# Adaptive layer norm of the head in six shares of channels in place of four

## The reference

```python
mod = jax.nn.silu(c) @ ada_w[i] + ada_b[i]            # ada_w is 2048 x 12288
sh1, sc1, g1, sh2, sc2, g2 = jnp.split(mod[:, None, :], 6, axis=-1)
mod_c = jax.nn.silu(c_ctx) @ ada_w[i] + ada_b[i]
...
h = modulate(rms_norm(x, norm1_g[i]), sh1, sc1)       # h * (1 + scale) + shift
hc = modulate(rms_norm(ctx, norm1_g[i]), csh1, csc1)
proj = h @ w_in[i]
```

## Time and profile before

| | |
|---|---|
| time, median of 3 runs (lowest to highest) | 1738.75 us (1736.94 to 1738.83) |
| the profiled execution: time, span in the trace | 1738.52 us, 1736.8 us |
| TensorE busy | 1684.4 us, 97% of the span |
| DVE busy, ACT busy | 1082.6 us, 752.5 us |
| DMA, mean over the span | 214 GB/s |
| DMA, 60 to 120 us | 386 to 387 GB/s |
| granted TensorE clock, mean | 0.987 |

### The profile page before, as it was taken

The page is one execution under the profiler, slowest core; times in us unless marked ns, Lnnn a source line. Parts: engine busy times, 40 slices in busy tenths (PEclk is TensorE's granted clock), DMA queues, the critical chain, the costliest instruction groups (busy, mean ns, idle before and its releaser), DMA issues.

```text
span 1736.8 us, 23807 instructions
## 1 busy us (share of the span) xinstructions
PE 1684.4 (97%) x8800; PEld 1377.5 (79%) x8800; DVE 1082.6 (62%) x1349; ACT 752.5 (43%) x960; POOL 108.7 (6%) x161
## 2 busy tenths in 40 slices
PE   4999999999999999999999899999999999999996
PEld 1468888888888678888888788888888888888885
DVE  1338777768786575554555666666666666655556
ACT  2233222623221565444444455555555555444444
POOL 0002222122121000000000000000000000000000
PEclk7999999999999999999999999999999999999998
DMA  9999888269795127666565566666666665565551
GB/s 354 387 386 335 305 292 284 76 233 326 238 316 195 51 79 262 192 187 191 191 241 189 152 182 187 188 191 185 191 192 185 191 191 185 192 193 193 194 192 63
DMA packets 161237, 371.53 MB, mean 214 GB/s; under 512 B 11607, under 2 KB 12359, under 8 KB 160022
## 3 DMA queue, kind: packets, MB, share of 16 engines
q1 hardware_dynamic: 139808, 291.98, 52.2%
q0 software_dynamic: 20144, 74.22, 12.5%
q10 hardware_dynamic: 1222, 4.47, 0.6%
HBM read 368.43 MB, written 2.21 MB: 213 GB/s over the span
## 4 chain that ended last, share of the span: by engine, by line
PE 92%; DMA 4%; DVE 2%; ACT 1%; issue 1%; SPq 0%; POOL 0%; ACTq 0%; DVEq 0%
PE ps L1833 21%; PE ps L1832 10%; PE ps L1842 10%; PE ps L1844 10%; PE ps L1843 10%; PE ps L2218 4%; PE ps L2219 4%; PE ps L2220 4%; DMA raw<-in_ada_w 4%; PE ps L1757 3%; PE ps L1758 3%; PE ps L1759 3%; PE ps L1829 1%; PE ps L1749 1%; PE ps L1911 1%; PE ps L1893 1%
## 5 line engine op out<-in xcount | busy, mean ns | idle before, releaser
L1127 DVE TENSOR_TENSOR w_lo<-raw,w_hi 128x1024 fp32r<-128x1024 f32 x480 | 584.7, 1224 | 431.7 <-ACT w_hi L669 431.2
L669 ACT CAST w_hi<-raw 128x1024 fp32r<-128x1024 f32 x480 | 503.4, 1050 | 771.4 <-PE ps L1844 273.8
L1833 PE MATMUL ps<-h2T,w_hi 128*128 128x512 f32 x1320 | 463.0, 394 | 0.0
L1832 PE MATMUL ps<-h2T,w_lo 128*128 128x256 f32 x1320 | 366.9, 278 | 0.0
L1833 PEld LDWEIGHTS ps<-h2T,w_hi 128*128 128x128 f32 x1320 | 247.9, 188 | 53.6
L1832 PEld LDWEIGHTS ps<-h2T,w_lo 128*128 128x128 f32 x1320 | 248.4, 188 | 4.2
L1842 PE MATMUL ps<-w_hi,hT 128*128 128x512 f32 x512 | 202.5, 395 | 0.0
L1201 DVE SCALAR_TENSOR_TENSOR ada_acc<-ada_raw,silu_c,ada_acc 128x512 f32<-128x512 f32 x240 | 180.0, 750 | 32.3 <-DMA ada_raw<-in_ada_w 16.9
L1844 PE MATMUL ps<-w_hi,hT 128*128 128x512 f32 x512 | 199.4, 390 | 0.0
L1843 PE MATMUL ps<-w_lo,hT 128*128 128x512 f32 x512 | 199.4, 389 | 0.0
L2218 PE MATMUL ps<-w_hi,f_hi 128*128 128x512 f32 x352 | 137.0, 389 | 1.0 <-DVE conv_in L1578 1.0
(11 more groups left out here) (222 smaller groups left out, 1920.0 us busy)
## 6 DMA issues: line engine op xcount, KB each, us to landing
raw<-in_ffn_w_up SPq DMA_DIRECT2D x176, 512.0 KB, 3.8
raw<-in_w_in SPq DMA_DIRECT2D x152, 512.0 KB, 4.8
ada_raw<-in_ada_w POOLq DMA_DIRECT2D x128, 512.0 KB, 6.1
raw<-in_ffn_w_down SPq DMA_DIRECT2D x88, 512.0 KB, 4.2
raw<-in_ada_w SPq DMA_DIRECT2D x64, 512.0 KB, 10.6
raw<-in_w_out SPq DMA_DIRECT2D x32, 512.0 KB, 3.9
raw<-in_w_branch_a SPq DMA_DIRECT2D x16, 512.0 KB, 3.7
raw<-in_w_branch_b SPq DMA_DIRECT2D x16, 512.0 KB, 3.6
```

Source lines behind the costliest of these rows:

```text
L669: act.copy(w_hi[:, s % SPLIT_SLOTS, :], raw[:, s, :]).then_inc(hi_ready[s], 1)
L1127: dve.tensor_tensor(w_lo[:, s % SPLIT_SLOTS, :], raw[:, s, :], w_hi[:, s % SPLIT_SLOTS, :], ALU.subtract).then_inc(lo_ready[s], 1)
L1832: pe.matmul(ps[:, b + t, 0:SEQ], w_lo[:, row4(s), at], high(kc), start=False, stop=False)
L1833: mm = pe.matmul(o, w_hi[:, row4(s), at], both(kc), start=False, stop=(kc == KC - 1))
```

## The change

The shares become six, of 2, 4, 4, 2, 2 and 2 channel groups. A unit of a share of four is as it was. A unit of a share of two takes two groups of weight rows: two DMAs of 256 KB, each of 256 columns of shift and 256 of scale per weight row, into the same slot of `raw`; a share of two has 8 units, so there are 64 units as before, and 32 more DMAs. The four strips of PSUM then hold shift and scale of two channel groups for the even and the odd weight rows, and `turn_mod` adds the two halves with a matmul by `pair_sum` (98 rows by 34 columns, made once by DVE) in place of the transpose. The order of K loads, K tiles, turns of tokens and sums is written anew: K loads stand ahead of the units in `K_LOADS`, and behind the last unit come two tiles of slot 6 and all of slot 7, where before it were the last two tiles of slot 5 and all of slots 6 and 7.

```diff
-QUARTERS = 4
-SHARE = KC // QUARTERS
-K_AFTER = (3, 10)
-           (5, 0): (3, 11), (5, 1): (3, 12), (5, 2): (3, 15), (5, 3): (3, 15)}
+SHARES = (2, 4, 4, 2, 2, 2)
+FIRST_KC = [sum(SHARES[:q]) for q in range(len(SHARES))]
+SHARE_OF = [q for q, n in enumerate(SHARES) for _ in range(n)]
+ROWS_OF = [2 if n == 2 else 1 for n in SHARES]
+UNITS_OF = [KC // n for n in ROWS_OF]
+K_LOADS = {(1, 2): 0, (2, 2): 1, (2, 9): 2, (3, 1): 3, (3, 4): 4, (4, 3): 5, (5, 3): 6}
+           (3, 0): (3, 5), (3, 1): (3, 6), (3, 2): (4, 0), (3, 3): (4, 1),
...
-                    sp.dma_start(raw[:, n % SLOTS, :].rearrange("p (a n) -> p a n", a=2),
-                                 shift_scale[:, kc, :, GROUP * q:GROUP * (q + 1)]).then_inc(raw_landed[n % SLOTS], 16)
+                    cols = slice(P * FIRST_KC[q], P * (FIRST_KC[q] + SHARES[q]))
+                    dst = raw[:, n % SLOTS, :].rearrange("p (k a n) -> p k a n", k=ROWS_OF[q], a=2)
+                    for k in range(ROWS_OF[q]):
+                        sp.dma_start(dst[:, k, :, :], shift_scale[:, ROWS_OF[q] * u + k, :, cols])\
+                            .then_inc(raw_landed[n % SLOTS], 16)
...
-            pool.wait_ge(mod1_ready, QUARTERS)
+            pool.wait_ge(mod1_ready, len(SHARES))
...
-            for q in range(QUARTERS):
-                if q:
-                    head_hi(2 * q - 1)
+            for q, n in enumerate(SHARES):
                 read_mod_rows(q)
-                if q == QUARTERS - 1:
-                    head_hi(2 * q)
-                for kc in range(SHARE * q, SHARE * q + 2):
+                if q == len(SHARES) - 1:
+                    head_hi(SLOTS - 1)
+                for kc in range(FIRST_KC[q], FIRST_KC[q] + n):
                     modulate(kc)
-                head_hi(2 * q + 1 if q == QUARTERS - 1 else 2 * q)
-                for kc in range(SHARE * q + 2, SHARE * q + 4):
-                    modulate(kc)
+                    if kc % 2 and kc < KC - 1:
+                        head_hi(kc // 2)
...
+            dve.tensor_tensor(pair_sum[:], consts[0:PIECE_AT[-1] + 2, 0:PIECE_AT[1] + 2],
+                              consts[0:PIECE_AT[-1] + 2, PIECE_AT[2]:PIECE_AT[-1] + 2], ALU.add)\
+                .then_inc(vecs_ready, 1)
...
-                    mm = pe.transpose(ps[:, MOD_BANK, 32 * PIECES * n:32 * PIECES * n + rows],
-                                      mod_rows[:, q % 2, n * P:(n + 1) * P], consts[0:rows, 0:rows])
+                    at, columns = PIECES * 32 * n, mod_rows[:, q % 2, n * P:(n + 1) * P]
+                    if SHARES[q] == 4:
+                        mm = pe.transpose(ps[:, MOD_BANK, at:at + rows], columns, consts[0:rows, 0:rows])
+                    else:
+                        mm = pe.matmul(ps[:, MOD_BANK, at:at + PIECE_AT[1] + 2], columns, pair_sum[:],
+                                       start=True, stop=True)
...
-                pe.wait_ge(raw_landed[slot], 16 * (n // SLOTS) + 16)
+                pe.wait_ge(raw_landed[slot], 16 * landings(q, u))
                 for n, at in enumerate(PIECE_AT):
+                    kc = u if SHARES[q] == 4 else 2 * u + n // 2
                     mm = pe.matmul(ps[at:at + 32, ADA_BANKS[q], 0:PIECE], c_pair[:, 2 * kc:2 * kc + 32],
...
+                if q and u == 0:
+                    turn_mod(q - 1)
...
-                        if (s, t) in ((1, 1), (3, 1), (5, 2)):
-                            turn_mod(q)
-                if kc == 14:
-                    turn_tokens(SHARE * q)
-                if q and kc in (2, 4, 5):
-                    turn_tokens(SHARE * (q - 1) + {2: 1, 4: 2, 5: 3}[kc])
-            turn_tokens(KC - 3)
+                if u == UNITS_OF[q] - 2:
+                    turn_tokens(FIRST_KC[q])
+                if q:
+                    for n, behind in ((1, 2), (2, 4), (3, 5)):
+                        if u == behind and n < SHARES[q - 1]:
+                            turn_tokens(FIRST_KC[q - 1] + n)
+            head_k(SLOTS - 2, 2)
+            turn_mod(len(SHARES) - 1)
+            head_k(SLOTS - 2, 3)
+            turn_tokens(KC - 1)
+            take(0, SLOTS - 1)
```

More of the change, by code:

```diff
@@ L73 @@
                ("k", KB), ("q", QB), ("v", VB), ("q", QB + GROUP), ("k", KB + GROUP), ("v", VB + GROUP)]
-QUARTERS = 4
-SHARE = KC // QUARTERS
-K_AFTER = (3, 10)
-K_TILES = {(0, 0): (1, 6), (0, 1): (1, 8), (0, 2): (1, 10), (0, 3): (1, 12),
[5 rows of a table removed]
-def head_units():
[L94 to L99, removed]
+SHARES = (2, 4, 4, 2, 2, 2)
[4 more added lines that the diff above has]
+K_LOADS = {(1, 2): 0, (2, 2): 1, (2, 9): 2, (3, 1): 3, (3, 4): 4, (4, 3): 5, (5, 3): 6}
+K_TILES = {(0, 0): (1, 7), (0, 1): (1, 8), (0, 2): (1, 10), (0, 3): (1, 12),
[6 rows of a table added]
+def head_units():
+    units = []
+    for q in range(len(SHARES)):
+        for u in range(UNITS_OF[q]):
+            if (q, u) in K_LOADS:
+                units.append(("k", K_LOADS[q, u]))
+            units.append(("ada", q, u))
+    return units + [("k", SLOTS - 1)]
 HEAD = head_units()
 ADA_UNITS = [unit for unit in HEAD if unit[0] == "ada"]
-ADA_BANKS = (0, 4, 5, 4)
+ADA_BANKS = [4 * (q > 0) + (q - 1) % 2 * (q > 0) for q in range(len(SHARES))]
 PIECES = 4
@@ L111, in loads_before, with units_until, landings @@
 def loads_before(j):
-    return len(ADA_UNITS) // SLOTS + j
+    return sum(ROWS_OF[q] for _, q, _ in ADA_UNITS) // SLOTS + j
+def units_until(q):
+    return sum(UNITS_OF[:q + 1])
+def landings(q, u):
+    return sum(ROWS_OF[n] * UNITS_OF[n] for n in range(q)) // SLOTS + ROWS_OF[q] * (u // SLOTS + 1)
 def turn_bank(kc):
@@ L258, in block_program @@
     mod_rows = place("mod_rows", att, [PIECE_AT[-1] + 2, 2, PIECE])
+    pair_sum = place("pair_sum", att + 4 * kb, [PIECE_AT[-1] + 2, PIECE_AT[1] + 2])
     x2 = place("x2", att, [P, TOK, D])
@@ L737, in read_mod_rows @@
                 b = ADA_BANKS[q]
-                act.wait_ge(ada1_used, KC * (q + 1))
+                act.wait_ge(ada1_used, units_until(q))
                 if q >= 2:
@@ L1261, in _ @@
             norm_tokens(3)
-            for q in range(QUARTERS):
-                if q:
-                    head_lo(2 * q - 1)
+            for q, n in enumerate(SHARES):
                 modulation1(q)
-                if q == QUARTERS - 1:
-                    head_lo(2 * q)
-                for kc in range(SHARE * q, SHARE * q + 2):
+                if q == len(SHARES) - 1:
+                    head_lo(SLOTS - 1)
+                for kc in range(FIRST_KC[q], FIRST_KC[q] + n):
                     split_modulated(kc)
-                head_lo(2 * q + 1 if q == QUARTERS - 1 else 2 * q)
-                for kc in range(SHARE * q + 2, SHARE * q + 4):
-                    split_modulated(kc)
+                    if kc % 2 and kc < KC - 1:
+                        head_lo(kc // 2)
             for s in range(2):
@@ L1721, in turn_tokens @@
                     pe.wait_ge(modulated_ready, 2 * (kc - 1))
-                if kc % SHARE == 1:
-                    pe.wait_ge(mod1_ready, kc // SHARE + 1)
+                if kc == FIRST_KC[SHARE_OF[kc]] + 1:
+                    pe.wait_ge(mod1_ready, SHARE_OF[kc] + 1)
                 for t in range(2 * TOK):
@@ L1784, in _ @@
             pe.transpose(ps[:, 2, 0:89], param_rows[0:89, 5, :], consts[0:89, 0:89]).then_inc(vecs_turned, 1)
-            for _, q, kc in ADA_UNITS:
-                unit_ada(q, kc)
-                if (q, kc) == (1, 1):
-                    turn_mod(0)
+            for _, q, u in ADA_UNITS:
+                unit_ada(q, u)
+                if q and u == 0:
+                    turn_mod(q - 1)
                 for (s, t), behind in K_TILES.items():
-                    if behind == (q, kc):
+                    if behind == (q, u):
                         if (s, t) == (0, 0):
@@ L1795, in _ @@
                         head_k(s, t)
[L1796 to L1811 removed]
+                if u == UNITS_OF[q] - 2:
[9 more added lines that the diff above has]
+            take(0, SLOTS - 1)
+            for i in range(2):
+                pe.wait_ge(hT_ready, KC - 1 + i)
+                for t in range(TILES):
+                    mm = products_k(SLOTS - 1, t, 0, KC - 2 + i, i)
+            mm.then_inc(used[SLOTS - 1], 1)
             def sum_mod(g, j):
```

46 lines of the change are left out of this document (23 added, 23 removed), and 9 rows, old and new, of the table K_TILES.

## The result

| | before | after |
|---|---|---|
| time, median (lowest to highest), 5 runs each | 1738.75 us (1736.94 to 1740.07) | 1745.49 us (1744.06 to 1746.39) |
| ratio to before, 95% interval | | 1.0040 [1.0029, 1.0051] |
| the profiled execution: time, span | 1738.52 us, 1736.8 us | 1746.12 us, 1744.4 us |
| unit 46 starts | 87.20 us | 89.67 us |
| job 1 starts | 132.95 us | 139.92 us |

What follows compares the result with a forecast made beforehand. TensorE bounds the kernel, so what counts is when job 1, the second projection, starts. Later loads 0.64, 1 KB rows 1.96, new wait 1.8 and work -0.3 sum to +4.1 us: 1743.0 us, range 1739.5 to 1747.5.

Steps and rivals of the forecast that it cites:

- likeliest case: Whole kernel: slower by the summed terms of the head, +4.1 us to 1743.0 us, bounds 1740.5 to 1745; chance 0.50.
- (c): By job 1: POOL's late loads of the other adaLN weights make DVE stand up to 4 us; 1745 us, chance 0.12.
- (d): Units 25 to 30: the lighter stretch lowers TensorE's clock, eight tiles cost 1.5 us more each; 1750 us, chance 0.06.
- What bounds the kernel: Head: landings set the time up to unit 43, then TensorE's work to job 1; any shift carries to the end.
- The meeting place and the arrival: At unit 46 the same work remains in both kernels; it waits for its landing and comes 2.6 us later.
- The four loads more and the 1 KB rows: Ahead of unit 46: 51 loads where 47 stood, 0.64 us; fourteen small units at 0.14 us each, 1.96 us.
- The DMAs' number: SP issues 32 more DMAs; its lead of eight units and its waits for free slots hide them.
- The new wait for w_lo of slot 6: Slot 6's first tile: TensorE stands 1.8 us, a 3.50 us chain covered by three units, 1.7 us at most.
- From unit 46 to job 1: The rest behind unit 46, 45.75 us before: +1.8 us for a new wait, -0.3 us for work.
- Work: Behind unit 46: one more turn_mod (0.33 us), one turn of tokens fewer (0.6 us), -0.3 us; pair_sum products no dearer.
- Rival (a): Tail: job 1 follows the landing of unit 64, so the kernel gets faster, 1733.9 us with free rows; chance 0.08.
- Rival (b): No measurable difference: 1 KB rows cost little and the new wait is shorter, 2.1 to 3.0 us, 1741.3 us; chance 0.24.

Runs made afterwards that it cites:

- kernel 8: The kernel before, four shares kept, with K loads, K tiles and turns of tokens and sums placed anew: 1737.62 us, ratio to before 0.9995.
- experiment 3: The kernel before with each adaLN unit read by two 256 KB DMAs with rows of 1 KB: 1745.18 us, ratio to before 1.0038.
- experiment 6: The changed kernel with slot 0's four K tiles moved back to units 23, 24, 26 and 28: 1745.17 us, ratio to before 1.0042.
- experiment 5: The changed kernel with the small shares' sums turned by the old 98-column transposes, not products with pair_sum: 1743.97 us, ratio to before 1.0033.
- kernel 7: The changed kernel with shares 4, 4, 4, 2, 2 and K loads, K tiles, token turns placed anew: 1736.21 us (0.9985), again 1734.22 us (0.9978).
- experiments 2: The changed kernel with small shares read in rows of 2 KB, same DMAs and bytes: 1744.07 us, ratio to before 1.0030.
- experiment 4: The kernel before with each adaLN unit read by two 256 KB DMAs with rows of 2 KB: 1738.57 us, ratio to before 0.9998.

## Why the prediction was right, and where it was short

It named slower as the likeliest, 1743.0 us with 1739.5 to 1747.5, and the measured 1745.49 lies inside, 2.5 us above the number. It is 0.5 us above the bounds of the likeliest case itself (1740.5 to 1745): the range holds it because it was made wide for rivals (c) and part of (d). Direction and place were foreseen; that the number is inside is partly luck. Its steps one by one:

- What bounds the kernel: right. What the head lost was carried to the end, 6.97 us at job 1 and 7.6 in the span; from job 1 to the end the two differ by 0.63 us, within the 1 us that I gave. It does not hold as closely everywhere: the same stretch is 1605.0 us in kernel 8 and 1605.9 in the profile of experiment 3, against 1603.85 before.
- The meeting place and the arrival: right. Unit 46 waits for its landing and starts at 89.67 us, forecast 89.8; the waits for `raw` stand in share 2 (59.03 us) and up to unit 46 (83.81, 88.17 and 89.67 us), none behind. The four loads more and the 1 KB rows were put at 0.64 and 1.96 us; taking the short rows away moved unit 46 by 2.08, so 0.39 of the 2.47 us is left for the loads. The rate fell from 387 to 353 GB/s, 9.6% dearer a byte, where I took 10% from the delivered rates and had 0 and 14% as bounds. The Trainium skill, "DMA: Bandwidth & Descriptors", section "Why small descriptors are slow (HBM only)", has the direction right; its overhead, by which I estimated 4.5%, is half of what these runs show. The DMAs' number, which I took as hidden behind SP's lead, cost nothing.
- The new wait for w_lo of slot 6: right in place and cause, 2.15 us for 1.8. I had let three units cover 1.7 us; between the end of the turn and the end of the units there were 1.5.
- From unit 46 to job 1: this is the part that failed in size. The sum had +1.5 and it is +4.50. Two terms of it were wrong. The clock was put at nothing in the likeliest case, and the one fall behind the wait is 1.53 us, by experiment 6; the same sum with 1.5 more would have come to about 1 us below the median. The other is "Work: one more turn_mod (0.33 us) and one turn of tokens fewer behind unit 46 (0.6 us): -0.3", with "the products over 34 columns stay within the 98-column transposes they replace": three `pair_sum` turns at 1.29 us stand for two of transposes at 0.38, so 0.91 where 0.33 was booked, and experiment 5 gives 0.73 of it back; one turn of tokens fewer is -0.41 (eight took 4.18 us, seven 3.77). With the wait at 2.15 and the wait for hT at -0.07 that makes 4.11. The 0.39 us left stand in the starts of the same 19 units and 20 tiles, which are that much further apart; I did not break them down further.
- Rival (a), the tail behind the last landing sets the time: no. No unit behind 46 waits for a landing in the change. Rival (b), no measurable difference: no, since the rows are not free. Rival (c), POOL's late loads hold DVE: no. DVE's first step on them, at 137.92 us, waited for nothing; the 0.63 us behind job 1 stand at `scores`. Rival (d), the clock: its mechanism came, but not as I put it. It did not fall in the light stretch as a whole but after single pauses of 2 us, for 3 us at a time. At 60 us the fall cost nothing that I can see, since unit 46 still waits for its landing; at 125 us it lies behind unit 46, where no wait takes it up. The trace of the kernel before had such a case, and I overlooked it: the clock is at 0.50 from 49 to 52 us, just behind waits of 1.48 and 0.72 us for landings.

The cause, then: of the 6.97 us at job 1 some 2.1 are the short rows ahead of unit 46, 2.9 the place of one turn of tokens (with the clock fall that follows the pause in the profiled execution), 0.7 the form of the turns of sums. The other 1.2 us, among them the loads that stand ahead of unit 46, no run takes away by itself. None of it has to be paid for having six shares: the same six, placed anew, are at 0.9988 of before, no slower. That is not to say that they are as good as five; beside kernel 7 they are 2.8 us slower, for reasons that stay partly open.

What stays open is when a pause of 2 us brings the clock down; I have the cases, not the rule.

## What to carry to other kernels

When a pipeline is cut into finer pieces, ask first what each finer piece does to the length of its rows in DRAM, and put the finer pieces where the landings no longer set the time: here at the end (kernel 7) rather than at the start. Then walk each chain that the finer cut makes (turn, ACT, DVE, next product) and count the work that lies between its ends in the new order; one turn placed one unit too late cost 2.9 us, more than the 2.1 of all the short rows. And judge a new cut only with its steps placed anew, or what is measured is the placing.

## What the runs showed of the hardware that I had not expected

- Rows of 1 KB are read at 352 to 354 GB/s where rows of 2 KB come at 386 to 387, and it makes no difference whether 512 KB come in one DMA or in two of 256 KB.
- A float32 product of 98 rows by 34 columns costs TensorE more than a transpose over 98 columns: 0.36 to 0.47 us for a pair of them against 0.11 to 0.17 in experiment 5.
- Pauses of TensorE of about 2 us are followed by some 3 us at the lower clock in some cases (2.05 us at 57 to 59 us and 2.15 us at 121 to 123 us of the change; 2.03 us at 592 to 594 us of the kernel before) and not in others (2.14 us in experiments 2 and 6; 2.03 us in experiment 4 and kernel 7). Shorter waits close together came before a fall as well: 1.48 and 0.72 us in the kernel before, 0.95 and 0.62 us in the first profile of kernel 7, whose second profile has 0.40 and 0.62 us there and no fall. On the path a fall costs 1.5 to 1.7 us: a wait of 2 us there is to be reckoned at up to 4.
- The granted clock can read 1.00 while the matmuls run at half speed: a unit takes 1.08 us up to 42 us in the change, as it does where the clock reads 0.50, and 0.64 us later on.
